# A gMLP layer with its MLP on one Trainium2 core: two more blocks of the MLP's input transposed by VectorE instead of TensorE, one combination moved to GpSimd, and two norm weights loaded later

## What is computed

```python
def rms_norm(x, g):
    return x * rsqrt(mean(x * x, axis=-1) + 1e-6) * g

h = rms_norm(x, norm1_g)
z = gelu(h @ a_w_in)                       # 1024 x 4096
u, v = split(z, 2)                         # 2048 columns each
v = layer_norm(v) * a_ln_g
sv = einsum('gts,nsge->ntge', tril(a_ws), v_in_chunks_of_128) + a_bs
y = x + (u * sv) @ a_w_out                 # the layer's middle result, 1024 x 1024
h = rms_norm(y, norm2_g)
y = y + square(relu(h @ mlp_w1)) @ mlp_w2  # 4096 hidden columns
return rms_norm(y, final_g)
```

## Time and profile before

| | us |
|---|---|
| median of 3 runs (lowest, highest) | 1124.45 (1124.19, 1124.59) |
| the profiled execution | 1126.03 |
| its span, from the first to the last recorded instruction | 1124.20 |
| PE busy in it | 1114.8 (99%) |
| DVE busy | 785.9 (70%) |
| ACT busy | 569.4 (51%) |
| POOL busy | 23.5 (2%) |

### The profile page before, as it was taken

How to read it: one execution, slowest core, us unless ns; L and a number is a source line. 1 busy time by engine, 2 the same in 40 slices (tenths; PEclk the granted TensorE clock), 3 DMA queues, 4 the chain that set the end, 5 groups by cost and what they waited for, 6 DMA issues and landing times.

```text
span 1124.2 us, 13090 instructions
## 1 busy us (share of the span) xinstructions
PE 1114.8 (99%) x5088; PEld 928.2 (83%) x5088; DVE 785.9 (70%) x833; ACT 569.4 (51%) x870; POOL 23.5 (2%) x17
## 2 busy tenths in 40 slices
PE   8999999999999999999999999999999999999997
PEld 7888888888888888888888888888888888888886
DVE  4976655688779986678658547455599575677666
ACT  6774444553554334565774365454653433433456
POOL 0000000000000000000000000000000000000240
PEclk9999999999999999999999999999999999999999
DMA  8173253272865494731353635527878354343213
GB/s 294 45 210 127 94 187 113 75 244 93 316 250 221 159 358 144 217 113 38 113 187 126 211 113 183 193 108 272 293 292 305 111 226 187 113 150 113 78 73 150
DMA packets 81933, 193.80 MB, mean 172 GB/s; under 512 B 4528, under 2 KB 10704, under 8 KB 75216
## 3 DMA queue, kind: packets, MB, share of 16 engines
q1 hardware_dynamic: 81392, 192.69, 48.7%
q10 hardware_dynamic: 480, 0.28, 0.1%
HBM read 134.24 MB, written 58.72 MB: 172 GB/s over the span
## 4 chain that ended last, share of the span: by engine, by line
PE 98%; DMA 1%; ACT 0%; DVE 0%; ACTq 0%; issue 0%
PE banks L427 32%; PE banks L432 32%; PE banks L431 32%; PE banks L496 3%; PE banks L541 1%; DMA gain_rows<-in_a_ln_g_dram 1%; DVE rows L1516 0%; ACT spare L1133 0%; PE banks L503 0%; PE banks L552 0%; PE banks L523 0%; ACT rows L1325 0%; ACT o_rms L1333 0%; ACTq L922 0%; ACTq L924 0%
## 5 line engine op out<-in xcount | busy, mean ns | idle before, releaser
L984 ACT ACTIVATE pair_high<-left_and_right 128x1024 fp32r<-128x1024 f32 x168 | 177.2, 1060 | 244.4 <-PE banks L427 193.4
L1378 DVE TENSOR_TENSOR ring_low<-left_and_right,ring_high 128x512 fp32r<-128x512 f32 x224 | 152.6, 692 | 192.7 <-ACT ring_high L954 192.3
L1386 DVE TENSOR_TENSOR pair_low<-left_and_right,pair_high 128x1024 fp32r<-128x1024 f32 x168 | 204.1, 1230 | 113.9 <-ACT pair_high L984 113.9
L954 ACT ACTIVATE ring_high<-left_and_right 128x512 fp32r<-128x512 f32 x224 | 138.4, 629 | 251.2 <-PE banks L427 155.9
L427 PE MATMUL banks<-pair_high 128*128 128x512 f32 x672 | 261.9, 390 | 0.0
L432 PE MATMUL banks<-pair_high,pair_low 128*128 128x512 f32 x672 | 261.5, 389 | 0.0
L431 PE MATMUL banks<-pair_low,pair_high 128*128 128x512 f32 x672 | 261.4, 389 | 0.0
L427 PE MATMUL banks<-s_high,ring_high 128*128 128x512 f32 x384 | 149.6, 389 | 0.0
L431 PE MATMUL banks<-s_low,ring_high 128*128 128x512 f32 x384 | 149.4, 389 | 0.0
L432 PE MATMUL banks<-s_high,ring_low 128*128 128x512 f32 x384 | 149.4, 389 | 0.0
L427 PEld LDWEIGHTS banks<-pair_high 128*128 128x128 f32 x672 | 126.1, 188 | 26.6 <-DVE pair_low L1386 0.3
(11 more groups left out here) (116 smaller groups left out, 1223.5 us busy)
## 6 DMA issues: line engine op xcount, KB each, us to landing
left_and_right<-sums SPq DMA_DIRECT2D x40, 1024.0 KB, 7.1
left_and_right<-in_mlp_w_dram SPq DMA_DIRECT2D x36, 1024.0 KB, 6.5
sums<-rows SPq DMA_DIRECT2D x34, 1024.0 KB, 5.4
left_and_right<-in_a_w_in_dram SPq DMA_DIRECT2D x19, 1024.0 KB, 6.2
v_blocks<-rows SPq DMA_DIRECT2D x8, 1024.0 KB, 4.5
left_and_right<-in_a_w_out_dram SPq DMA_DIRECT2D x8, 1024.0 KB, 9.7
rows<-in_x_dram SPq DMA_DIRECT2D x7, 1024.0 KB, 8.7
spare<-v_blocks SPq DMA_DIRECT2D x6, 1024.0 KB, 6.9
```

Of the source, the lines that this page charges most:

```text
L954: nc.scalar.activation(ring_high[k][:, :], right_place(n, pos)[:, k, :], ACT.Copy)\
L984: nc.scalar.activation(pair_high[pair_entry(d, pos, k)][:, :, :], pair_of(d, pos, k), ACT.Copy)\
L1378: nc.vector.tensor_tensor(ring_low[k][:, :], right_place(n, pos)[:, k, :], ring_high[k][:, :].bitcast(F32), ALU.subtract).then_inc(low_don ...
L1386: nc.vector.tensor_tensor(pair_low[e][:, :, :], pair_of(d, pos, k), pair_high[e][:, :, :].bitcast(F32), ALU.subtract).then_inc(low_done, 1)
```

## The change

What it does, part by part:
- PE's `turn` for single 4 is gone, and so are ACT's `evict_turned` for it. c11 and c21 are moved within SBUF by `move_quads`: 16 DMAs each, of 32 partitions and 64 KB, issued by SP; then `turn_y` on DVE, at the end of double 0 for a12 and after `sum_t(4, 1)` in single 4 for a22. The second norm weight is applied where the turned block is read: on ACT in the high part (`high_turned`, four instructions), on DVE in the low part (`low_turned`, four) and in the combinations s2 and s4 (`sum_turned`, four each in place of one).
- raw_s3 is computed by GpSimd in one instruction.
- a12, s2 and a22 of single 4 are split in four steps, and PE waits for each step.
- `add_rows(0, 6)` moves from after the four ring splits of single 4's first position to between the second and the third.
- All of mlp_w1 is loaded in the order of fours; the PE-transposed norm2_g is gone. a_ln_g and norm2_g in fours are loaded by SP after the bias, and a_ln_g is transposed in single 1, before `turn_ws`, into one more bank.

```diff
-                pe.wait_ge(gains_landed, 32)
-                begin_fill("gains", 7)
+            def turn_gains():
+                pe.wait_ge(gains_landed, 16)
+                bank = other_set(1)[1]
+                begin_fill("gains", bank)
+                nc.tensor.transpose(ps[:, bank, 0:JT], gain_rows[:, :], ident[0:JT, 0:JT]).then_inc(full[bank], 1)
...
-                        if n == 4 and pos == 0 and k == 1:
-                            turn(4, "a22", set_of(slot(4, 1)))
                         if pos == 2 and k == 2 and n == 1:
+                            turn_gains()
                             turn_ws()
...
-                        if d == 0 and pos == 6 and k == 5:
-                            turn(4, "a12", set_of(slot_double(0, 5)))
...
-            turn_gains()
             warm(3)
...
+            def move_quads(b, blk, dst):
+                y_final(sp, blk)
+                for q in range(4):
+                    for r in range(4):
+                        sp.dma_start(dst[32 * q:32 * q + 32, r:4 * QT:4, :],
+                                     block_of[blk][32 * r:32 * r + 32, :, P * q:P * q + P])\
+                          .then_inc(quads_landed[b], 16)
...
-                    load_quads("a21", "c22", quad)
-                    y_final(sp, "c11")
+                    load_quads("a21", "c22", quad_a21)
+                    sp.wait_ge(low_done, unit_double(0, 5, 7) + 1)
+                    move_quads("a12", "c11", quad_a12)
                     sp.dma_start(y_of("c11"), block_of["c11"]).then_inc(y_stored["c11"], 16)
                     sp.wait_ge(low_done, unit_double(0, 6, 3) + 1)
                     load_weight(4, "b12")
                     sp.wait_ge(low_done, unit_double(0, 6, 7) + 1)
                     load_weight(4, "b22")
-                    y_final(sp, "c21")
+                    move_quads("a22", "c21", quad_a22)
                     sp.dma_start(y_of("c21"), block_of["c21"]).then_inc(y_stored["c21"], 16)
...
+            def high_turned(s):
+                act.wait_ge(y_turned, {"a12": 3, "a22": 4}[s])
+                if s == "a12":
+                    act.wait_ge(unit_begun, done(unit_double(0, 6, 5)))
+                for k in range(4):
+                    nc.scalar.activation(high[s][:, k, :], raw_of[s][:, k, :], ACT.Copy,
+                                         scale=g2_fours[:, 0, k:k + 1]).then_inc(combo_high, 1)
...
                 elif n == 4:
-                    high_combo(4, "a12")
+                    high_turned("a12")
                     split_high(4, 1, 0)
-                    evict_turned(4, "a22", set_of(slot(4, 1)))
                     split_high(4, 1, 1)
...
+            def sum_turned(s):
+                if s == "s2":
+                    dve.wait_ge(y_turned, 4)
+                    dve.wait_ge(s3_pooled, 1)
+                    out, left, right = raw_s2, raw_a22, raw_s3
+                else:
+                    dve.wait_ge(combo_sum, combo_sum_count(4, "s1"))
+                    out, left, right = raw_s4, raw_a12, raw_s2
+                for k in range(4):
+                    nc.vector.scalar_tensor_tensor(out=out[:, k, :], in0=left[:, k, :], scalar=g2_fours[:, 0, k:k + 1],
+                                                   in1=right[:, k, :], op0=ALU.mult, op1=ALU.subtract)\
+                      .then_inc(combo_sum, 1)
...
                 elif n == 4:
-                    add_rows(0, 6)
-                    low_combo(4, "a12")
+                    low_turned("a12")
                     sum_t(4, 0)
-                    split_low(4, 1, 0)
-                    split_low(4, 1, 1)
-                    sum_combo(4, "s2")
-                    split_low(4, 1, 2)
-                    split_low(4, 1, 3)
+                    for k in range(4):
+                        split_low(4, 1, k)
...
                 sum_t(n, 1)
+                if n == 4:
+                    turn_y("a22")
+                    sum_turned("s2")
+                    low_step(4, "s2", 0)
                 split_low(n, 2, 0)
                 if n == 4:
-                    low_combo(4, "s2")
+                    low_step(4, "s2", 1)
                 split_low(n, 2, 1)
+                if n == 4:
+                    low_step(4, "s2", 2)
-                if n in (0, 4):
-                    sum_combo(n, "s1")
                 split_low(n, 2, 2)
+                if n == 4:
+                    low_step(4, "s2", 3)
+                    sum_combo(4, "s1")
                 split_low(n, 2, 3)
...
                     if pos == 6 and d == 0:
-                        sum_combo(4, "s3")
+                        turn_y("a12")
                     for k in range(4):
+                        if pos == 6 and d == 0 and k == 2:
+                            add_rows(0, 6)
...
+            pool.wait_ge(y_scaled, 8)
+            nc.gpsimd.tensor_tensor(raw_s3[:, :, :], raw_a11[:, :, :], raw_a21[:, :, :], ALU.subtract)\
+              .then_inc(s3_pooled, 1)
```

More of the change, by code:

```diff
@@ L35 @@
 COMBOS = ["a12", "s2", "s1", "s3", "s4", "a22"]
+STEPPED = {0: [], 4: ["a11", "a12", "s2", "a22"]}
 REGIONS = ["a11", "a12", "a22", "s2", "s3", "s4", "s1"]
@@ L291, in trunk @@
         g2_landed = sem("g2_landed")
-        quads_landed = {b: sem(f"quads_landed_{b}") for b in ("a11", "a21", "a12")}
+        quads_landed = {b: sem(f"quads_landed_{b}") for b in ("a11", "a21", "a12", "a22")}
         y_turned = sem("y_turned")
         y_scaled = sem("y_scaled")
+        s3_pooled = sem("s3_pooled")
         v_stored = {b: sem(f"v_stored_{b}") for b in BLOCKS}
@@ L1016, in scale_y @@
             def scale_y(blk):
-                i, raw = {"a11": (0, raw_a11), "a21": (1, raw_a21), "a12": (2, raw_a12)}[blk]
+                i, raw = {"a11": (0, raw_a11), "a21": (1, raw_a21)}[blk]
                 act.wait_ge(g2_landed, 16)
@@ L1272, in double @@
                         square_rows(0, "c11", y_sq, y_squared)
-                    if pos == 6 and d == 0:
-                        evict_turned(4, "a12", set_of(slot_double(0, 5)))
                     for k in range(4):
@@ L1312, in _ @@
             first_high(3)
[L1313 removed]
+            evict_turned("a11", set_of(1))
             for n in range(4):
```

149 lines of the change are left out of this document (78 added, 71 removed).

## The result

| us | before | after |
|---|---|---|
| median of 5 runs each (lowest, highest) | 1124.45 (1124.19, 1124.63) | 1128.77 (1127.97, 1130.02) |
| the profiled execution | 1126.03 | 1127.97 |
| its span | 1124.20 | 1126.30 |
| PE busy in it | 1114.8 | 1112.4 |

The ratio of the medians is 1.0039, with a 95% interval of 1.0025 to 1.0054: the changed kernel is slower by 4.3 us, more than the 0.2% that the measurement of this kernel can tell. The forecast was 1126.6, the range 1122.2 to 1129.6. So the range held the time, the direction was right, and the size was half of what came; the forecast lay just inside of 0.2%, the result lies outside of it.

What follows compares the result with a forecast made beforehand. PE was taken to bound the kernel, carrying 98% of the chain; -0.74 + 0.1 - 3.5 + 2.0 + 2.2 + 1.7 + 0.4 = +2.15 us on the median 1124.45 gave 1126.6, range 1122.2 to 1129.6.

Steps and rivals of the forecast that it cites:

- Start: First product of the kernel: without PE's wait for a_ln_g, PE starts 0.74 us earlier and what follows moves along.
- The clock at the start: Half-clock stretch from 9.50 to 12.70 us: bounds 0 and -1.7 us, taken as 0.
- the clock stays up: Rival: no half clock at the start, with the long hold; +0.45 us, 1124.9; chance 0.12.
- Removed transposes: Single 4's left operands: two groups of 16 transposes leave PE, 1.75 us each, -3.5 us.
- The hold before the last unit: Last unit of double 0: GpSimd's new instruction holds off DVE's low part, 2.0 us of idle PE.
- the long one: Before double 0's last unit: GpSimd holds DVE off for its whole length; ends of the term 0 and 2.4 us.
- Before single 4: Before single 4's first unit: DVE's transpose of a12 delays the ring's first low part, 2.2 us idle PE.
- Before position 2: Position 2 of single 4: the listed work takes 12.55 us against four units' 10.88, 1.7 us idle PE.
- Before position 3: Behind position 2 of single 4: DVE's work ends about 11.2 us after its begin, against 10.88; 0.4 us idle.
- The clock falls in the middle: Rival: half clock behind the new idle times costs 1.7 us; +3.85, 1128.3; chance 0.08.
- late moves: Rival: second set of moves delays a22's transpose in single 4; +3.65 us together, or +5.5; chance 0.12.
- The moves: SP's two sets of 16 DMAs, 0.48 us per issue, land in time for DVE's transposes; cost nothing.

Runs made afterwards that it cites:

- e3: The kernel before, unchanged, profiled once more: 1124.69 us.
- e4: The kernel before with only a11 - a21 (s3) moved to GpSimd, at once after the scaling of a21: 1124.88 us, ratio 1.0000.
- e1: The kernel before with only the late loads and the gains' transpose in single 1; single 4's transposes stay on PE: 1124.30 us, ratio 0.9995.
- e5: The changed kernel with s3 on GpSimd in four pieces of 512 columns instead of one instruction: 1126.61 us, ratio 1.0009.
- e11: The changed kernel again, without any edit: 1128.54 us, ratio 1.0033 against the kernel before.
- e2: The changed kernel, GpSimd's s3 waiting until DVE has written the low part of double 0's last unit: 1126.27 us, ratio 1.0009.
- e8: The changed kernel with s3 back on DVE, before the transpose of a12, nothing on GpSimd: 1127.19 us, ratio 1.0017.
- e7: e2 with other orders of DVE's and ACT's work around position 2 of single 4: 1123.83 us, ratio 0.9990.
- e9: e7 with GpSimd's s3 in four pieces beside DVE's one-input work, a11's last low part later: 1122.54 us, ratio 0.9979.

## Why the prediction came out as it did

**Start, −0.74: too large.** The first step was right (the wait for a_ln_g goes, the ring's low part is next), but the size came from an execution in which that load was later than in the other two profiles with this start: 1.78 us of wait, against 1.18 in e3 and 1.10 in e4. And what follows does not simply move along, as the prediction had it: in the changed kernel's profile the first product begins at 8.38, 0.49 ahead of e3, then PE waits 0.46 us at 26.45 for ACT's raw_a, and at 479 us the lead is gone (479.10 against 479.05). At full clock the whole part is worth nothing in e1's median. The forecast set the term against the profiled execution and then carried the sum over to the median of the runs, as if both had had the same start. They hadn't: the profiled one had the half clock, and the five runs of the comparison, all below 1124.7, by their times had not. The 1.58 us between them was named in the prediction and passed over; it was the sign of this.

**The clock at the start, 0: a question wrongly put.** The rival "the clock stays up" could not gain anything against a median that had no half clock in it.

**Removed transposes, −3.5: right.** 32 instructions fewer on PE.

**The hold before the last unit, +2.0: right**, measured 2.07 both times. Of the two ends the long one held: the hold lasts for the whole instruction of GpSimd, shown at 128x512 (e5) and 128x2048 (after, e4), with GpSimd's length 4.60 to 4.62 where I had 4.6. The Trainium skill says in "SBUF - State Buffer", section "Who interferes with whom", that a DVE instruction with two SBUF inputs contends with a GpSimd instruction that reads SBUF, under an exclusive lock, and that one with a single SBUF input does not. Both halves agree with the traces: pair_low 4.80 instead of 1.22, the transpose 3.91 beside GpSimd.

**Before single 4, +2.2: right**, 2.12 in e11. With the half clock behind the first idle time (after) it is 0.61, "largely swallowed" as the rival had it.

**Before position 2, +1.7: 0.3 too small**, 1.98 to 2.0. The terms that the prediction lists there add up to 11.8 us; its 12.55 is reached only with the 0.69 of the ring's low part itself, which the list leaves out. **Before position 3, +0.4: right** to 0.15.

**The clock falls in the middle, a rival at 0.08: too small by far.** It gave +3.85 and 1128.3, against 1128.77 and 1128.54. This is the step that failed, and the only one whose price is large: I had the row that shows a half clock behind 1.75 us idle, wrote that three idle times of that size arise, and still took the clock as staying up. By the sum and the clocks above it falls where nothing swallows it in most executions of after, e2 and e5, and in half of e8's. That the range held the time all the same is owed to its upper end, which was drawn for late moves and not for this: the clock's rival ended at 1128.3, below both medians.

**The moves, 0: right, with the wrong pitch.** 0.65 us per issue where I had 0.48, and 2.0 to landing: 15 x 0.65 + 2.0 = 11.7 us against the 11.6 that I had for the second set. The 1.6 us to spare were none. It wasn't late in after, where DVE was later too; in e2 it was, by 0.23.

Put together for e11 against the lower hump: start 0 to −0.3, transposes −3.5, idle times +6.4, clock +1.7: +4.3 to +4.6, measured 4.2. The forecast had −0.64 for start and gains, −3.5 and +6.3. So the 2.1 us by which +2.15 fell short of the measured 4.2 are 1.7 from the clock and the rest from the start.

Why the change doesn't pay: PE carried the end, but in the last 2.7 us of double 0 and the first 25 us of single 4 DVE had no slack, so work taken off PE there comes back as a wait for DVE: 3.5 us taken off, 6.4 us idle. DVE's transpose (3.8 to 3.9 us) is twice as long as PE's sixteen (1.75). But most of the 6.4 is the order of the work and not the transposes themselves: GpSimd one unit later takes it to 3.8 (e2), another order around position 2 to 2.9 (e7), GpSimd's pieces beside one-input work to 1.5 (e9). e9 shows that the same transposes can be made to pay 1.8 us, when GpSimd's reads lie beside one-input work and DVE serves the ring before the combinations.

## What to carry to other kernels

A busy share of 70% says nothing about a stretch: before work is moved to an engine, add up what it must deliver unit by unit at the very place, and with it what starts on GpSimd while that engine's two-input operations are due. An idle time that is new on TensorE is to be charged with a stretch at half clock behind it, with a real chance and not a small one, as soon as the trace shows one of that length to be followed by it. And before a profiled execution is used for a sum, ask why it is longer than the median; a part of the sum may belong to that execution alone.

## What was not expected of the hardware

- **The granted clock.** Every profile ends with a stretch at 0.50 behind its last matmul, which costs nothing. All others that the profiles show are 3.4 us long (503.3 to 506.7 in after, 529.0 to 532.4 in e2). They followed idle times of 1.75 us (before), 2.07 (after), 2.3 (e2) and 2.12 with 2.07 shortly before it (e11). Behind 2.07 alone (e11, first), 2.15 (e5), 2.94 (e8, windows above) and the 1.98 to 2.0 before position 2 in after, e5, e8 and e11 the clock stayed at 1.00. So no length of idle time alone tells whether it falls; what else decides, these runs leave open.
- **Small moves within SBUF.** 16 DMAs of 32 partitions and 64 KB were issued by SP at 0.65 us each in both sets, and at 0.65 and 0.68 in e2 (10.80 us for the 16 of its second set), where loads of 256 KB from DRAM took 0.48. Each landed after 2.0 us.
- **DVE beside GpSimd.** DVE's transpose of 128x2048 in 3.91 us against 3.81, and four adds of PSUM and SBUF in 2.46 against 2.48, with GpSimd reading two SBUF tiles all the while (e2) or nearly all of it (e9); GpSimd itself took 4.94 us beside the transpose, 4.60 to 4.62 while it held DVE off.
